# Low parts of weights taken from GpSimd after the first stage, softmax weighting moved to VectorE, three staggered steps in the attentions of a three-layer fp32 block

## The chip, the cores and the metric

One core of a Trainium2 chip runs the whole program in one launch. The metric is the device time in microseconds (us), the median of three runs of the kernel before.

## The reference

256 tokens of width 1024 go through two blocks in fp32. Three attentions and three feed-forward parts are computed, each on a normed residual:

```python
# first block: 16 heads in 8 pairs
y_b = mla_attention(q_nope, q_rope, k_nope, k_rope, v_b)     # 8 heads, 256 keys, causal
y_a = dsa_sparse_attention(...)                              # 8 heads, keys chosen by top-k of an index score, bias by distance
x = x + (gates0 * (y_a @ w_branch_a) + gates1 * (y_b @ w_branch_b)) @ w_out
x = x + square(relu(rmsnorm(x) @ w_ff1)) @ w_ff2             # 4096 wide
# second block, two layers
h = h + swa_sink_mixer(...)     # 16 heads, window of 128, a bias by distance, a sink: P = softmax(S)
h = h + swiglu(...)             # 2816 wide
h = h + nsa_mixer(...)          # 16 heads, three softmaxes each: compressed, selected, window; gated sum
h = h + swiglu(...)
```

## The kernel before

**Weights.** All weights stream through SBUF as 292 slabs of 128 x 1024 fp32, in the order of `_schedule`. Every product of a weight is made of three matmuls of fp32r parts: high part with high part, low with high, high with low. So each slab is split twice before TensorE reads it: its high part (a rounding copy, `hi <- stage`), and its low part (`lo <- stage - hi`, written over the stage). Six double slots of `stage` and eight slots of `hi` turn over. Who splits which slab is set by two sets of slab numbers: `HI_BY_DVE` (VectorE; all others ScalarE) and `LO_BY_POOL` (GpSimd; all others VectorE). Before, VectorE makes the high parts of slabs 20 to 38, 118 to 128, 217, 219, 221 and 223, and GpSimd the low parts of 6 to 38, 112, 114 to 128, the even ones from 194 to 212, and 214 to 225.

**When a split is made.** Each engine's program is an instruction list written out by hand, and runs in order. Class `Splits` keeps its place in it: `slabs.splits(n)` first makes the low parts that are due (`flush`), then up to n high parts of slabs whose slot has been given back; their low parts fall due at the next call. Low parts thus follow one call behind the high ones.

**The three attentions** work on pairs of heads, ten iterations p = 0 to 9 for eight pairs, with the work of neighbouring pairs interleaved. In `pairs` (first and windowed attention) TensorE makes the scores of pair p (`products`), VectorE adds the bias and takes the row maximum (`top`, writes P), ScalarE takes the exponential and its row sum, VectorE inverts the sum, ScalarE multiplies P by it (L1339, the weighting), TensorE transposes the P of pair p - 1 (`turn`), ScalarE copies it to the slot PT (`pt`, L1347), TensorE multiplies the PT of pair p - 2 with the values (`by_values`), and ScalarE and VectorE split the output (`OTH`, `OTL`). Between these stand three calls `fill(p, 0..2)`, which put parts of weight tiles between the steps of the attention: a tile (24 matmuls) has three parts, the first with 6 matmuls, the second with 6, the last with 12; the ScalarE and VectorE programs take the finished tile out of its bank in the third part (`ZR`, `QS` or `AQ <- bank`). Two banks (2 and 3) take turns for these tiles in the first two attentions, one bank (7) in the third; TensorE can't start a tile before VectorE has read the one that last stood in the bank. The fill of the first attention calls `splits(2)` at i = 0 and 2, the fills of the others `splits(1)` at i = 0 and 2.

In the third attention (`nsa_products`, `nsa_turn`, `nsa_values`; scores in `nsa_scores`, weighting on VectorE already in `nsa_weights`, L2249) each pair has six score blocks.

**The bias table of the first attention.** VectorE makes a mask from the top-k at the end of iteration 2 (`MASK`). GpSimd waits for it, then issues eight DMAs that load the bias B1, and then evaluates a flag (`choose`); VectorE's `top` of pair 4 waits for that (`b1`). GpSimd's queue holds the low parts of slabs 24 and on behind it.

Of the kernel before, what the change touches and what calls it, by code (L numbers as in the profile page):

```python
# [318 lines left out]
def _program(nc, io, sched):  # L319
# [70 lines left out]
    PTA = work("PTA", [128, 3, 384], F32, 69632)  # L390
# [30 lines left out]
    PTB = work("PTB", [128, 3, 384], F32, 67008)  # L421
# [11 lines left out]
    PTN = work("PTN", [128, 2, 768], F32, 28672)  # L433
    PCT = work("PCT", [64, 2, 256], F32, 34816)
# [35 lines left out]
    HI_BY_DVE = {*range(20, 39), *range(118, 129), 217, 219, 221, 223}  # L470
    LO_BY_POOL = {*range(6, 39), 112, *range(114, 129), *range(194, 213, 2), *range(214, 226)}
# [25 lines left out]
    def tensor(e):  # L497
# [264 lines left out]
        def pairs(name, P, PT, starts, products, value, fill, also=lambda p: None):  # L762

            def turn(p):
                for h in (2 * p, 2 * p + 1):
                    b = 4 + h % 2
                    clear(b)
                    for part in range(2):
                        q.wait_ge(*at("probabilities", name, h, part))
                    for i, c in enumerate(starts):  # L770
                        x = e.transpose(bank[b][:, 128 * i:128 * i + 128], P[:, h % 4, c:c + 128], idc[:, 0:128])
                    x.then_inc(*up("turned", ("turned", name, h)))
                    free[b] = [("pt", name, h)]

            def by_values(p):
                b, out = 6 + p % 2, bank[6 + p % 2]
                clear(b)
                for o in range(2):
                    q.wait_ge(*at("pt", name, 2 * p + o))
                v = [value(2 * p + o) for o in range(2)]  # L780
                for key in v[0][2]:
                    q.wait_ge(*at(*key))
                for i in range(2):
                    for o, (x, c, _) in enumerate(v):
                        y = e.matmul(out[HALF[o], 128 * i:256], x[:, i, c:c + 64], PT[:, o, 256 * i:256 + 128 * i], start=i == 0, stop=i == 1)
                y.then_inc(*up("values", ("values", name, p)))
                free[b] = [("o high", name, p), ("o low", name, p)]

            for p in range(10):
                if p < 8:  # L790
                    products(p)
                    free[0], free[1] = [("scores read", name, 2 * p)], [("scores read", name, 2 * p + 1)]
                fill(p, 0)
                if p >= 2:
                    by_values(p - 2)
                fill(p, 1)
                if 1 <= p < 9:
                    turn(p - 1)
                fill(p, 2)
                also(p)  # L800
# [211 lines left out]
        def nsa_values(p):  # L1012
            g_, out = p // 4, bank[6]
            clear(6)
            for o in range(2):
                for i in range(2):
                    q.wait_ge(*at("ptn", 2 * p + o, i))
            q.wait_ge(*at("slc values"))
            q.wait_ge(*at("win values"))
            for v, c in ((VS3, 0), (VW3, 384)):  # L1020
                for i in range(2):
                    for o in range(2):
                        x = e.matmul(out[HALF[o], 128 * i:256], v[:, i, 64 * g_:64 * g_ + 64], PTN[:, o, c + 256 * i:c + 256 + 128 * i], start=c + i == 0, stop=False)  # L1023
# [15 lines left out]
        for p in range(10):  # L1039
            if p < 8:  # L1040
                nsa_products(p)
            filler.parts(attention_parts(p, NSA_PARTS)[0])
            if p >= 2:
                nsa_values(p - 2)
            if 1 <= p < 9:
                nsa_turn(2 * p - 2)
            filler.parts(attention_parts(p, NSA_PARTS)[1])
            if 1 <= p < 9:
                nsa_turn(2 * p - 1)
            filler.parts(attention_parts(p, NSA_PARTS)[2])  # L1050
            if p == 0:
                compressed_values()
# [26 lines left out]
    def scalar(e):  # L1079
# [243 lines left out]
        def pairs(name, P, PT, blocks, starts, fill, also=lambda p: None):  # L1323

            for p in range(10):
                if p < 8:
                    for h in (2 * p, 2 * p + 1):
                        for i, (c, w) in enumerate(blocks):
                            exponential(P[:, h % 4, c:c + w], h % 4, i, [("top", name, h, i)], ("exp", name, h, i))
                fill(p, 0)  # L1330
                if p >= 2:
                    q.wait_ge(*at("values", name, p - 2))
                    out_free(name)
                    e.activation(OTH[:, out_tile(name, p - 2), :], bank[6 + p % 2][:, 0:256], ACT.Copy).then_inc(*up("high", ("o high", name, p - 2), ("high", name + " out", out_tile(name, p - 2))))
                if p < 8:
                    for h in (2 * p, 2 * p + 1):
                        q.wait_ge(*at("inverse", name, h))
# [3 lines left out]
                if 1 <= p < 9:  # L1341
                    for o in range(2):
                        h = 2 * p - 2 + o
                        q.wait_ge(*at("turned", name, h))
                        if h >= 2:
                            q.wait_ge(*at("values", name, p - 2))
                        e.activation(PT[:, o, :], bank[4 + o][:, 0:384], ACT.Copy).then_inc(*up("pt", ("pt", name, h)))  # L1347
                fill(p, 2)
                also(p)
# [22 lines left out]

        pairs("first", PA, PTA, ((0, 256), (256, 128)), (256, 0, 128), first_fill, first_also)

# [71 lines left out]
        def attention_fill(p, i, more):  # L1446
            filler.parts(attention_parts(p, more)[i])
            if i != 1:
                slabs.splits(1)
# [6 lines left out]
        pairs("swa", PB, PTB, ((0, 258), (258, 129)), (258, 0, 130), lambda p, i: attention_fill(p, i, SWA_PARTS), swa_also)  # L1456
# [90 lines left out]
        def nsa_turn(h):  # L1547
            q.wait_ge(*at("nsa turned", h, 0))
            if h >= 2:
                q.wait_ge(*at("ptn read", h // 2 - 1))  # L1550
            e.activation(PTN[:, h % 2, 0:512], bank[4][:, :], ACT.Copy).then_inc(*up("pt", ("ptn", h, 0)))
# [5 lines left out]
            e.activation(PTN[:, h % 2, 512:768], bank[5][:, 0:256], ACT.Copy).then_inc(*up("pt", ("ptn", h, 1)))  # L1557

        for p in range(10):
            if p < 8:  # L1560
# [7 lines left out]
            if 1 <= p < 9:  # L1568
                nsa_turn(2 * p - 1)
            attention_fill(p, 2, NSA_PARTS)  # L1570
# [31 lines left out]
    def vector(e):  # L1602
# [367 lines left out]
        def pairs(name, P, blocks, ready, fill, also=lambda p: None):  # L1970
            for p in range(10):
# [9 lines left out]
                if p < 8:  # L1981
                    for h in (2 * p, 2 * p + 1):
                        c = 72 + 6 * (h % 4)
                        q.wait_ge(*at("exp", name, h, 1))
                        e.reciprocal(small[:, c:c + 2], small[:, c:c + 2]).then_inc(*up("step", ("inverse", name, h)))
                if p >= 2:
                    out_low(name, p - 2, 6 + p % 2)
                fill(p, 1)
# [43 lines left out]
        pairs("first", PA, first_blocks, first_ready, first_fill, first_also)  # L2032
# [70 lines left out]
        def attention_fill(p, i, more):  # L2103
# [3 lines left out]
            if i != 1:  # L2107
                slabs.splits(1)
# [5 lines left out]
        pairs("swa", PB, lambda h: ((0, 258, BT[:, h, 0:258]), (258, 129, BT[:, h, 130:259])), swa_ready, lambda p, i: attention_fill(p, i, SWA_PARTS))  # L2114
# [146 lines left out]
        for p in range(10):  # L2261
# [9 lines left out]
            if p < 8:  # L2271
                nsa_weights(2 * p + 1)
            attention_fill(p, 2, NSA_PARTS)
# [20 lines left out]
    def gpsimd(e):  # L2294
# [200 lines left out]
        def attention(more):  # L2495
            for p in range(10):
                for i in range(3):
                    filler.parts(attention_parts(p, more)[i])
                    if i != 1:
                        slabs.splits(1)  # L2500
# [4 lines left out]
        attention(SWA_PARTS)  # L2505
# [44 lines left out]
        attention(NSA_PARTS)  # L2550
# [134 lines left out]
```

## Time and profile before

| | |
|---|---|
| median of 3 runs | 1016.66 us (1015.15 to 1017.91) |
| the profiled execution | 1016.81 us; its span, first to last instruction, 1014.5 us; 2.3 us lie around it |
| TensorE matmul busy | 963.8 us, 95% of the span |
| VectorE / ScalarE / GpSimd busy | 650.6 / 543.5 / 303.6 us |
| mean granted TensorE clock | 0.977 |
| stages, us from the span's start | first projections 0 to 72; first attention 72 to 155; to 400 its output, projection and feed-forward; windowed attention 400 to 462; third-layer projections 662 to 711; third attention 711 to 800 |

Read first where TensorE is not busy, then who released it after each wait, then what that engine did before. Rows of the timeline have start, duration, engine, line and operation, out <- in, the count of instructions merged in a row, and in brackets the idle time ahead with its releaser. L numbers are lines of the kernel.

### The profile page before, as it was taken

What the parts mean: (1) busy time and instruction counts of PE and PEld (TensorE: products, weight loads), DVE (VectorE), ACT (ScalarE), POOL (GpSimd) and SP (SyncE); (2) the same over time, 40 slices, a digit from 0 to 9 for tenths busy, and PEclk for the clock granted to TensorE, in tenths of its full rate; (3) what the DMA queues carried; (4) which work ended last, traced back from release to release, by engine and by line L of the source; (5) the groups of instructions that cost most, each with busy time, mean ns of one, the idle gap of its engine ahead of it and who ended that gap; (6) DMA issues with size and microseconds to landing.
All of it is one profiled execution on the core that took longest, in us unless ns stands there. A gap on an engine that the chain in (4) does not pass through costs nothing.

```text
span 1014.5 us, 19347 instructions
## 1 busy us (share of the span) xinstructions
PE 963.8 (95%) x7816; PEld 929.5 (92%) x7816; DVE 650.6 (64%) x1354; ACT 543.5 (54%) x1136; POOL 303.6 (30%) x202
## 2 busy tenths in 40 slices
PE   7859999999999999899999999998798999999997
PEld 7859899999999999789999999997676999999997
DVE  5897556675555555956865565666997377555552
ACT  6536453565445457676644444456678365444434
POOL 2756674210000015633121111427431022111111
PEclk8979999999999999999999999999799899999999
DMA  8783534495545544216954545455211254554521
GB/s 286 195 184 114 167 126 172 151 271 208 197 169 194 177 167 166 84 45 200 282 189 171 200 170 185 149 208 208 79 47 43 84 202 172 183 192 170 200 88 42
DMA packets 26536, 165.81 MB, mean 163 GB/s; under 512 B 3352, under 2 KB 4248, under 8 KB 8016
## 3 DMA queue, kind: packets, MB, share of 16 engines
q1 hardware_dynamic: 24048, 156.61, 44.1%
q0 software_dynamic: 2400, 7.97, 4.1%
q8 instruction: 62, 1.02, 0.4%
q14 instruction: 26, 0.21, 0.1%
HBM read 161.03 MB, written 3.01 MB: 162 GB/s over the span
## 4 chain that ended last, share of the span: by engine, by line
PE 81%; DVE 9%; ACT 5%; DMA 1%; issue 1%; POOL 1%; SPq 0%; DVEq 0%; POOLq 0%
PE bank L521 12%; PE bank L529 12%; PE bank L525 12%; PE bank L558 9%; PE bank L562 9%; PE bank L560 9%; PE bank L532 4%; PE bank L533 4%; PE bank L538 2%; PE bank L536 2%; DVE DG L1878 1%; ACT PN L1321 1%; DVE PN L2249 1%; DVE hi L1613 1%; PE bank L1023 1%
## 5 line engine op out<-in xcount | busy, mean ns | idle before, releaser
L1089 ACT ACTIVATE hi<-stage 128x1024 fp32r<-128x1024 f32 x257 | 264.6, 1045 | 51.3 <-PE bank L562 47.1
L1620 DVE TENSOR_TENSOR lo<-stage,hi 128x1024 fp32r<-128x1024 f32 x220 | 269.5, 1257 | 12.5 <-ACT hi L1089 12.4
L2302 POOL TENSOR_TENSOR lo<-stage,hi 128x1024 fp32r<-128x1024 f32 (+1 forms) x71 | 177.3, 2516 | 275.3 <-ACT hi L1089 240.7
L558 PE MATMUL bank<-UH,hi 128*128 128x256 f32 x608 | 172.3, 283 | 0.0
L562 PE MATMUL bank<-UL,hi 128*128 128x256 f32 x608 | 172.2, 283 | 0.0
L560 PE MATMUL bank<-UH,lo 128*128 128x256 f32 x608 | 172.1, 283 | 0.0
L521 PE MATMUL bank<-HTH,hi 128*128 128x256 f32 (+1 forms) x1038 | 159.6, 290 | 13.1 <-DVE QS L1709 6.8
L529 PE MATMUL bank<-HTL,hi 128*128 128x256 f32 (+1 forms) x1038 | 157.6, 289 | 0.0
L525 PE MATMUL bank<-HTH,lo 128*128 128x256 f32 (+1 forms) x1038 | 156.5, 287 | 0.2 <-DVE lo L1620 0.2
L521 PEld LDWEIGHTS bank<-HTH,hi 128*128 128x128 f32 (+1 forms) x1038 | 138.8, 193 | 18.3 <-DVE QS L1709 7.6
L2521 POOL TENSOR_TENSOR TH<-TH,RR 128x256 f32<-128x256 f32 x44 | 68.1, 1549 | 279.9 <-DVE TH L2126 279.9
L529 PEld LDWEIGHTS bank<-HTL,hi 128*128 128x128 f32 (+1 forms) x1038 | 139.5, 194 | 2.0 <-issue 1.8
L525 PEld LDWEIGHTS bank<-HTH,lo 128*128 128x128 f32 (+1 forms) x1038 | 138.8, 194 | 1.1 <-issue 0.7
L562 PEld LDWEIGHTS bank<-UL,hi 128*128 128x128 f32 x608 | 116.7, 192 | 0.1
L558 PEld LDWEIGHTS bank<-UH,hi 128*128 128x128 f32 x608 | 116.7, 192 | 0.1
L560 PEld LDWEIGHTS bank<-UH,lo 128*128 128x128 f32 x608 | 116.7, 192 | 0.0
L532 PE MATMUL bank<-HTH,hi 128*128 128x256 f32 (+2 forms) x346 | 98.9, 286 | 0.0
L533 PE MATMUL bank<-HTH,lo 128*128 128x256 f32 (+2 forms) x346 | 98.7, 285 | 0.0
L1397 ACT ACTIVATE UH<-U 128x256 fp32r<-128x256 f32 x76 | 31.7, 417 | 82.8 <-DVE U L2132 81.8
L533 PEld LDWEIGHTS bank<-HTH,lo 128*128 128x128 f32 (+2 forms) x346 | 67.1, 194 | 0.0
L532 PEld LDWEIGHTS bank<-HTH,hi 128*128 128x128 f32 (+2 forms) x346 | 67.1, 194 | 0.0
L2064 DVE TENSOR_TENSOR UL<-U,UH 128x256 fp32r<-128x256 f32 x76 | 32.9, 433 | 51.3 <-ACT UH L1397 51.3
(310 smaller groups left out, 1549.5 us busy)
## 6 DMA issues: line engine op xcount, KB each, us to landing
stage<-in_stream SPq DMA_DIRECT2D x144, 1024.0 KB, 4.8
BT<-scratch POOLq DMA_DIRECT2D x8, 256.0 KB, 15.4
BT<-scratch POOLq DMA_DIRECT2D x4, 512.0 KB, 20.0
stage<-in_stream SPq DMA_DIRECT2D x3, 512.0 KB, 9.6
scratch<-VR POOLq DMA_DIRECT2D x2, 768.0 KB, 21.0
XT<-in_xt SPq DMA_DIRECT2D x4, 256.0 KB, 6.4
B<-scratch POOLq DMA_DIRECT2D x4, 256.0 KB, 5.2
out<-ROWS SPq DMA_DIRECT2D x4, 256.0 KB, 2.4
```

Source lines behind the costliest of these rows:

```text
L521: e.matmul(out, wh[k], rows.high(k0 + k), start=k == 0, stop=False)
L525: e.matmul(out, wl[k], rows.high(k0 + k), start=False, stop=False)
L529: e.matmul(out, wh[k], rows.low(k0 + k), start=False, stop=False)
L532: e.matmul(out, wh[k], rows.high(k0 + k), start=False, stop=False)
L533: e.matmul(out, wl[k], rows.high(k0 + k), start=False, stop=False)
L558: e.matmul(out, hi[:, j % HI_SLOTS, c:c + 128], rows.high(k), start=start and n % 2 == 0, stop=False)
L560: e.matmul(out, lo[:, j // 2 % ST_PAIRS, j % 2, c:c + 128], rows.high(k), start=False, stop=False)
L562: last = e.matmul(out, hi[:, j % HI_SLOTS, c:c + 128], rows.low(k), start=False, stop=stop)
L1089: e.activation(hi[:, j % HI_SLOTS, 0:w], stage[:, j // 2 % ST_PAIRS, j % 2, 0:w], ACT.Copy).then_inc(*up("hi", ("hi", j, 0)))
L1620: e.tensor_tensor(lo[x], stage[x], f32(hi[:, j % HI_SLOTS, 0:sched[j][2]]), ALU.subtract).then_inc(*up("lo", ("lo", j, 0)))
L2302: e.tensor_tensor(lo[x], stage[x], f32(hi[:, j % HI_SLOTS, 0:sched[j][2]]), ALU.subtract).then_inc(*up("lo_pool", ("lo", j, 0)))
L2521: e.tensor_tensor(t, z, ROOT[stage], ALU.mult).then_inc(*up("silu", ("silu scaled", kind, f)))
```

## The change

Slab by slab: `HI_BY_DVE` becomes empty (ScalarE makes all high parts), and GpSimd keeps the low parts of slabs 6 to 19 alone (VectorE makes the rest). In `pairs` the weighting of P moves from ScalarE (two activations for each head) to VectorE (two `tensor_scalar` for each head), right behind the inversion. In all three attentions the order becomes: scores, fill 0, transposes of the pair before, fill 1, values of the pair before that, fill 2; in the third, the first head's transposes stand ahead of the scores. Four PT slots instead of two used ones let the transposed P of a pair stand while the next is written. How many high parts each fill makes is read from a table in the second and third attention.

```diff
-    PTA = work("PTA", [128, 3, 384], F32, 69632)
+    PTA = work("PTA", [128, 4, 384], F32, 66560)
...
-    PTN = work("PTN", [128, 2, 768], F32, 28672)
-    PCT = work("PCT", [64, 2, 256], F32, 34816)
+    PTN = work("PTN", [128, 4, 768], F32, 28672)
+    PCT = work("PCT", [64, 2, 256], F32, 49280)
...
-    HI_BY_DVE = {*range(20, 39), *range(118, 129), 217, 219, 221, 223}
-    LO_BY_POOL = {*range(6, 39), 112, *range(114, 129), *range(194, 213, 2), *range(214, 226)}
+    SWA_SPLITS = ((0, 0, 1),) * 5 + ((0, 1, 1), (0, 1, 1), (1, 1, 1), (1, 1, 1), (1, 1, 1))
+    NSA_SPLITS = ((0, 0, 1),) * 6 + ((0, 1, 1), (0, 1, 1), (1, 1, 1), (1, 1, 1))
+
+    HI_BY_DVE = set()
+    LO_BY_POOL = set(range(6, 20))
# TensorE, pairs
                 fill(p, 0)
+                if 1 <= p < 9:
+                    turn(p - 1)
+                fill(p, 1)
                 if p >= 2:
                     by_values(p - 2)
-                fill(p, 1)
-                if 1 <= p < 9:
-                    turn(p - 1)
                 fill(p, 2)
# TensorE, third attention
         for p in range(10):
+            if 1 <= p < 9:
+                nsa_turn(2 * p - 2)
             if p < 8:
                 nsa_products(p)
             filler.parts(attention_parts(p, NSA_PARTS)[0])
+            if 1 <= p < 9:
+                nsa_turn(2 * p - 1)
+            filler.parts(attention_parts(p, NSA_PARTS)[1])
             if p >= 2:
                 nsa_values(p - 2)
-            if 1 <= p < 9:
-                nsa_turn(2 * p - 2)
-            filler.parts(attention_parts(p, NSA_PARTS)[1])
-            if 1 <= p < 9:
-                nsa_turn(2 * p - 1)
# ScalarE, pairs: the weighting goes
-                        for i, (c, w) in enumerate(((starts[1], starts[2] + 128 - starts[1]), (starts[0], 128))):
-                            e.activation(P[:, h % 4, c:c + w], P[:, h % 4, c:c + w], ACT.Copy, scale=row_stat(h % 4, 1, i)).then_inc(*up("pt", ("probabilities", name, h, i)))
# ScalarE, third attention: the turns stand ahead of each exponential
+            if 1 <= p < 9:
+                nsa_turn(2 * p - 2)
             if p < 8:
                 nsa_exp(2 * p)
-            attention_fill(p, 0, NSA_PARTS)
+            attention_fill(p, 0, NSA_PARTS, NSA_SPLITS)
             if 1 <= p < 9:
-                nsa_turn(2 * p - 2)
-            attention_fill(p, 1, NSA_PARTS)
+                nsa_turn(2 * p - 1)
+            attention_fill(p, 1, NSA_PARTS, NSA_SPLITS)
             if p < 8:
                 nsa_exp(2 * p + 1)
# VectorE, pairs
                         e.reciprocal(small[:, c:c + 2], small[:, c:c + 2]).then_inc(*up("step", ("inverse", name, h)))
+                        q.wait_ge(*at("inverse", name, h))
+                        for i, (c, w) in enumerate(((starts[1], starts[2] + 128 - starts[1]), (starts[0], 128))):
+                            e.tensor_scalar(P[:, h % 4, c:c + w], P[:, h % 4, c:c + w], row_stat(h % 4, 1, i), None, ALU.mult).then_inc(*up("probabilities", ("probabilities", name, h, i)))
+                fill(p, 1)
                 if p >= 2:
                     out_low(name, p - 2, 6 + p % 2)
-                fill(p, 1)
                 fill(p, 2)
# VectorE, third attention
-            attention_fill(p, 0, NSA_PARTS)
+            attention_fill(p, 0, NSA_PARTS, NSA_SPLITS)
+            if p < 8:
+                nsa_weights(2 * p)
+            attention_fill(p, 1, NSA_PARTS, NSA_SPLITS)
             if p >= 2:
                 outs(p - 2)
             if p < 8:
-                nsa_weights(2 * p)
-            attention_fill(p, 1, NSA_PARTS)
-            if p < 8:
                 nsa_weights(2 * p + 1)
```

## Rows read from the trace of the kernel before

**Rows 1.** Windows by stage: length, busy of each engine (instructions), granted clock, DMA, GB/s
```profile
72.00:155.00 83.00, 79.21 (x644) 72.68 (x643) 50.01 (x170) 47.89 (x147) 55.21 (x29) 1.00 0.44 145
...
400.00:462.00 62.00, 55.69 (x448) 49.67 (x447) 44.80 (x117) 44.39 (x136) 32.25 (x14) 0.97 0.26 94
...
662.00:711.00 49.00, 44.28 (x347) 40.81 (x347) 33.78 (x51) 27.88 (x45) 26.34 (x13) 0.97 0.59 214
711.00:800.00 89.00, 77.77 (x606) 65.50 (x605) 67.31 (x352) 59.25 (x241) 25.36 (x11) 0.90 0.14 49
```

**Rows 2.** Waits of TensorE: us in total, times, longest
```profile
PE bank L521 <- DVE QS L1709: 6.8, 4, 4.7
PE bank L785 <- ACT PTB L1347: 5.8, 4, 2.8
...
PE bank L934 <- POOL lo L2302: 2.1, 1, 2.1
...
PE bank L956 <- DVE HE L2200: 1.6, 1, 1.6
```

**Rows 3.** Five lines: ns min/median/max, first and last start
```profile
L1620 DVE TENSOR_TENSOR lo<-stage,hi x220: 710/1218/3405, 14.5 to 987.0; 128x1024 fp32r<-128x1024 f32 x109, 128x544 fp32r<-128x544 f32 x1
...
L1613 DVE CAST hi<-stage x34: 675/684/2867, 83.7 to 751.8; 128x1024 fp32r<-128x1024 f32 x34
...
L2249 DVE TENSOR_SCALAR PN<-PN,small x64: 272/313/2468, 716.9 to 785.5; 128x128 f32<-128x128 f32 x32, 128x256 f32<-128x256 f32 x32
...
L1692 DVE SCALAR_TENSOR_TENSOR XT<-XT,col,RR x8: 459/1718/2358, 410.9 to 427.9; 128x256 f32<-128x256 f32 x8
...
L1089 ACT ACTIVATE hi<-stage x257: 507/1045/1067, 13.4 to 982.8; 128x1024 fp32r<-128x1024 f32 x128, 128x544 fp32r<-128x544 f32 x1
```

**Rows 4.** Timeline of VectorE in the first attention
```profile
80.04 0.21 DVE L1985 RECIPROCAL small<-small 128x2 f32<-128x2 f32 x2
...
82.15 0.42 DVE L1709 TENSOR_TENSOR ZR<-bank,RR 128x256 f32<-128x256 f32 x1 [1.43 <-PE bank L538]
...
83.66 2.05 DVE L1613 CAST hi<-stage 128x1024 fp32r<-128x1024 f32 x2
...
115.32 0.42 DVE L1954 CUSTOM_DVE_ANT_0 PA<-bank,B 128x256 f32<-128x256 f32 x1 [6.53 <-POOL flag L2460]
...
118.29 0.41 DVE L1709 TENSOR_TENSOR ZR<-bank,RR 128x256 f32<-128x256 f32 x1
```

**Rows 5.** Timeline of GpSimd in the first attention
```profile
79.80 4.75 POOL L2302 TENSOR_TENSOR lo<-stage,hi 128x1024 fp32r<-128x1024 f32 x2 [3.47 <-ACT hi L1089]
...
101.46 4.64 POOL L2358 DMA_DIRECT2D B<-scratch  x8 [4.27 <-DVE MASK L2030]
```

**Rows 6.** Timeline of TensorE, windowed attention: scores of pairs 1, 3, 4 and 7
```profile
405.90 0.93 PE L808 MATMUL bank<-KW,QS 64*128 64x258 f32 x8
...
421.02 0.93 PE L808 MATMUL bank<-KW,QS 64*128 64x258 f32 x8
...
426.57 0.93 PE L808 MATMUL bank<-KW,QS 64*128 64x258 f32 x8
...
445.36 0.93 PE L808 MATMUL bank<-KW,QS 64*128 64x258 f32 x8
```

**Rows 7.** Timeline of VectorE in the third attention
```profile
716.85 3.09 DVE L2249 TENSOR_SCALAR PN<-PN,small 128x128 f32<-128x128 f32 x4
...
721.75 0.42 DVE L1709 TENSOR_TENSOR QS<-bank,RR 128x256 f32<-128x256 f32 x1
...
760.45 0.41 DVE L1709 TENSOR_TENSOR QS<-bank,RR 128x256 f32<-128x256 f32 x1
...
769.43 0.42 DVE L1709 TENSOR_TENSOR QS<-bank,RR 128x256 f32<-128x256 f32 x1
...
784.83 1.01 DVE L2249 TENSOR_SCALAR PN<-PN,small 128x128 f32<-128x128 f32 x4
```

**Rows 8.** Windows: one stretch at the lower clock
```profile
704.00:707.40 3.40, 3.40 (x18) 3.40 (x18) 0.56 (x1) 3.40 (x6) 3.07 (x2) 0.50 0.39 166
```

More of the change, by code:

```diff
@@ L420, in _program @@
     PB = work("PB", [128, 4, 388], F32, 59648)
-    PTB = work("PTB", [128, 3, 384], F32, 67008)
+    PTB = work("PTB", [128, 4, 384], F32, 67008)
     TH = work("TH", [128, 2, 2, 256], F32, 40960)
@@ L784, in by_values @@
                     for o, (x, c, _) in enumerate(v):
-                        y = e.matmul(out[HALF[o], 128 * i:256], x[:, i, c:c + 64], PT[:, o, 256 * i:256 + 128 * i], start=i == 0, stop=i == 1)
+                        y = e.matmul(out[HALF[o], 128 * i:256], x[:, i, c:c + 64], PT[:, (2 * p + o) % 4, 256 * i:256 + 128 * i], start=i == 0, stop=i == 1)
                 y.then_inc(*up("values", ("values", name, p)))
@@ L1022, in nsa_values @@
                     for o in range(2):
-                        x = e.matmul(out[HALF[o], 128 * i:256], v[:, i, 64 * g_:64 * g_ + 64], PTN[:, o, c + 256 * i:c + 256 + 128 * i], start=c + i == 0, stop=False)
+                        x = e.matmul(out[HALF[o], 128 * i:256], v[:, i, 64 * g_:64 * g_ + 64], PTN[:, (2 * p + o) % 4, c + 256 * i:c + 256 + 128 * i], start=c + i == 0, stop=False)
             x.then_inc(*up("values", ("ptn read", p)))
@@ L1321, in exponential, with pairs @@
             e.activation(P, P, ACT.Exp, bias=row_stat(slot, 0, i), scale=-1.0, accum_out=row_stat(slot, 1, i)).then_inc(*up("exp", done))
-        def pairs(name, P, PT, blocks, starts, fill, also=lambda p: None):
+        def pairs(name, P, PT, blocks, fill, also=lambda p: None):
             for p in range(10):
@@ L1330, in pairs @@
                 fill(p, 0)
+                if 1 <= p < 9:
+                    for h in (2 * p - 2, 2 * p - 1):
+                        q.wait_ge(*at("turned", name, h))
+                        if h >= 4:
+                            q.wait_ge(*at("values", name, p - 3))
+                        e.activation(PT[:, h % 4, :], bank[4 + h % 2][:, 0:384], ACT.Copy).then_inc(*up("pt", ("pt", name, h)))
+                fill(p, 1)
                 if p >= 2:
@@ L1371, in first_also @@
                 in_halves(("ak",), ZK, 0, AK, ("zk",), 0.125)
-        pairs("first", PA, PTA, ((0, 256), (256, 128)), (256, 0, 128), first_fill, first_also)
+        pairs("first", PA, PTA, ((0, 256), (256, 128)), first_fill, first_also)
         for i in range(8):
@@ L1444, in scalar, with attention_fill @@
                         + [(lambda i: part_of("swa_o", i, early), i) for m in ((4, 6), (0, 2)) for i in range(8 - STAG) for n in m])
-        def attention_fill(p, i, more):
+        def attention_fill(p, i, more, splits):
             filler.parts(attention_parts(p, more)[i])
-            if i != 1:
-                slabs.splits(1)
+            slabs.splits(splits[p][i])
         def swa_also(p):
@@ L1454, in swa_also @@
                 key_head(1)
-        pairs("swa", PB, PTB, ((0, 258), (258, 129)), (258, 0, 130), lambda p, i: attention_fill(p, i, SWA_PARTS), swa_also)
+        pairs("swa", PB, PTB, ((0, 258), (258, 129)), lambda p, i: attention_fill(p, i, SWA_PARTS, SWA_SPLITS), swa_also)
         project("swa_o", early, "mlp2", 4)
@@ L1548, in nsa_turn @@
             q.wait_ge(*at("nsa turned", h, 0))
-            if h >= 2:
-                q.wait_ge(*at("ptn read", h // 2 - 1))
-            e.activation(PTN[:, h % 2, 0:512], bank[4][:, :], ACT.Copy).then_inc(*up("pt", ("ptn", h, 0)))
+            if h >= 4:
+                q.wait_ge(*at("ptn read", h // 2 - 2))
+            e.activation(PTN[:, h % 4, 0:512], bank[4][:, :], ACT.Copy).then_inc(*up("pt", ("ptn", h, 0)))
             q.wait_ge(*at("nsa turned", h, 1))
@@ L1968, in flat_low, with pairs @@
             e.tensor_tensor(FLO[:, kv, :], FL[:, kv, :], f32(FH[:, kv, :]), ALU.subtract).then_inc(*up("low", ("flat low", kv)))
-        def pairs(name, P, blocks, ready, fill, also=lambda p: None):
+        def pairs(name, P, blocks, starts, ready, fill, also=lambda p: None):
             for p in range(10):
@@ L2030, in first_also @@
                 e.scalar_tensor_tensor(MASK[:, :], WKS[:, :], -1e30, causal, ALU.mult, ALU.min).then_inc(*up("step", ("mask",)))
-        pairs("first", PA, first_blocks, first_ready, first_fill, first_also)
+        pairs("first", PA, first_blocks, (256, 0, 128), first_ready, first_fill, first_also)
         assert rounds[0] == 8
@@ L2101, in vector, with attention_fill @@
                         + [(lambda i: part_of("swa_o", i, early), i) for m in ((4, 6), (0, 2)) for i in range(8 - STAG) for n in m])
-        def attention_fill(p, i, more):
+        def attention_fill(p, i, more, splits):
             filler.parts(attention_parts(p, more)[i])
@@ L2106, in attention_fill @@
                 some_later(1)
-            if i != 1:
-                slabs.splits(1)
+            slabs.splits(splits[p][i])
         def swa_ready(p):
@@ L2112, in swa_ready @@
             q.wait_ge(*at("bt"))
-        pairs("swa", PB, lambda h: ((0, 258, BT[:, h, 0:258]), (258, 129, BT[:, h, 130:259])), swa_ready, lambda p, i: attention_fill(p, i, SWA_PARTS))
+        pairs("swa", PB, lambda h: ((0, 258, BT[:, h, 0:258]), (258, 129, BT[:, h, 130:259])), (258, 0, 130), swa_ready, lambda p, i: attention_fill(p, i, SWA_PARTS, SWA_SPLITS))
         some_later(8)
@@ L2268, in vector @@
             if p < 8:
-                nsa_weights(2 * p)
-            attention_fill(p, 1, NSA_PARTS)
-            if p < 8:
                 nsa_weights(2 * p + 1)
-            attention_fill(p, 2, NSA_PARTS)
+            attention_fill(p, 2, NSA_PARTS, NSA_SPLITS)
         project("nsa_o", early, (7, 0, 1, 2), "mlp3", 6)
@@ L2493, in gpsimd, with attention @@
             slabs.splits(1)
-        def attention(more):
+        def attention(more, splits):
             for p in range(10):
@@ L2498, in attention @@
                     filler.parts(attention_parts(p, more)[i])
-                    if i != 1:
-                        slabs.splits(1)
+                    slabs.splits(splits[p][i])
         early = {}
@@ L2504, in gpsimd @@
                         + [(lambda i: part_of("swa_o", i, early), i) for m in ((4, 6), (0, 2)) for i in range(8 - STAG) for n in m])
-        attention(SWA_PARTS)
+        attention(SWA_PARTS, SWA_SPLITS)
         project("swa_o", early, "mlp2")
@@ L2549, in gpsimd @@
                         + [(lambda i: part_of("nsa_o", i, early), i) for n in (0, 2, 4) for i in range(8 - STAG)])
-        attention(NSA_PARTS)
+        attention(NSA_PARTS, NSA_SPLITS)
         project("nsa_o", early, "mlp3")
```

18 lines of the change are left out of this document (4 added, 14 removed).

## The prediction, made before the changed kernel ran

> **What bounds the kernel now.** First the windows by stage [rows 1]: TensorE is full but for 3.8 us in the first attention, 6.3 in the windowed one, 4.7 in the projections of the third layer and 11.2 in the third attention. Everywhere between 155 and 662 us but for the windowed attention it is full, so what a stage loses or wins there goes into the total whole. The clock column gives a second loss in the last three stages (0.97, 0.97, 0.90): one stretch of 3.4 us at the lower of the two levels, 1.2 GHz, stands by itself [rows 8], with 18 matmuls where a full stretch has twice as many; it follows two waits of 2.1 and 1.6 us. So an avoided wait can give back 1.7 us more than its length.
>
> Then the waits of TensorE [rows 2]. In the windowed attention it waits 5.8 us for ScalarE's PT copies; those stand in ScalarE's queue behind the weighting, and that behind VectorE. In the third layer it waits for one low part by GpSimd (2.1), for a tiny VectorE operation `HE` (1.6), and 6.8 us for VectorE's `QS` (4.7 of it once).
>
> Then why VectorE is late [rows 3]. Three of its operations have two durations: the cast of a slab 684 ns or up to 2867, the `tensor_scalar` of P 313 or up to 2468, the XT scaling 459 or a median of 1718. The long ones all overlap a low part by GpSimd (2.4 us each, [rows 5]): VectorE stands until GpSimd's operation is done. VectorE's sources in PSUM (`top`, `ZR`) don't show it.
>
> **What the change does, first attention.** It takes GpSimd out of the later stages, but here slabs 18 and 19 are still its own, at 79.80 to 84.55 [rows 5], and VectorE's new weighting of pair 0 would start right behind the inversion at 80.04 [rows 4]. So I expect the first `tensor_scalar` to stand until 82.2 and the second until 84.6; with the other two it is done at 85.5 (four take 1.01, [rows 7]), 5.2 later. The wait of 1.43 and the two casts of 2.05 that followed [rows 4] are no longer there: +1.8 for `top` of pair 1. In iteration 1 VectorE makes two low parts (1.22 each, [rows 3]) where it made two casts (0.68 each), and 1.0 of weighting: +2.1. The same in iteration 2, of which about 0.9 fills a wait for the exponential (an estimate): +1.2. Nothing of this was done by VectorE before, and all of it is ahead of the mask: GpSimd waits for the mask with nothing else to do (4.27 idle, [rows 5]), so mask, bias DMAs, flag and `top` of pair 4 are 5.1 us later. VectorE already stood 6.53 us for the flag [rows 4]; the whole chain shifts. Behind `top` of pair 4 stand two low parts and the weighting, 2.4 + 1.0, of which 1.5 replace waits and the OTL step that moves behind: the tile read `ZR` (118.29) comes another 1.9 later. TensorE's next tile needs that bank. It is full from there on, so it gets nothing back: **+7.0**. Bounds: 3, if pair 0's weighting doesn't meet GpSimd and the waits absorb more; 10, if ScalarE's 19 more high parts (1.05 each, [rows 3]) hold up the exponentials as well. With waits over 2 us in it, a stretch at the lower clock is likely: **+1** (0 to 3.4, two stretches as in [rows 8]).
>
> The Trainium skill has a rule that speaks against this move. By the Trainium skill, "SBUF — State Buffer", "SBUF: two separate sides", VectorE and GpSimd share a port pair that is an exclusive lock, and a VectorE operation in a two-port mode also keeps GpSimd from writing the descriptors of its own DMAs. The trace agrees on the lock (684 against 2867 ns); by the second half the eight bias DMAs could stretch under pair 3's weighting. No row here shows that, and the sum leaves it out.
>
> **Windowed attention.** GpSimd's 14 low parts go to VectorE (16 us by [rows 3]), the weighting too (8 pairs at 1.0). In return the 11 casts go (0.68 alone, up to 2.87), and the eight XT steps fall from 1.72 to 0.46, 10 us. VectorE, busy 44.8 of 62 [rows 1], stays about there. Before, pairs took 5.55 us where nothing was late (421.02 to 426.57, [rows 6]); the six from pair 1 to pair 7 took 39.5 (405.90 to 445.36). The PT copy of a pair now has a whole iteration, and P is needed one fill earlier, which VectorE alone can meet (weighting done some 4 us behind the scores). Six pairs at 5.55 are 33.3: **-6.2**. Bounds: -2, if low parts ahead of the weighting hold up the transposes; -8, with the lighter last pairs.
>
> **Ahead of the third attention.** The low part of a `cw1` slab comes 1.2 us after its high part instead of 2.4: -1.2 of the 2.1. `HE` no longer stands behind GpSimd: -1.6. The slow stretch goes: -1.7. **-4.5**; bounds -1 and -5.
>
> **Third attention.** Start: pair 0's weighting falls from 3.09 to 1.01 [rows 7], its gelu steps by about 1.1 (as `HE` in [rows 2], an estimate), and one low part, 1.2, comes in ahead: -2.0 for the first `QS`. Five iterations take 47.7 us (721.75 to 769.43, [rows 7]); the last of them, without a collision, takes 8.98. That is not VectorE's work but a loop: exponential of the first head, turn copies, exponential of the second head on ScalarE, then weighting and `QS`. The new order keeps this loop, now with a low part (1.2) in VectorE's gap, so I take 9.0 for each: 45.0, -2.7. In iterations 6 and 7 the table asks for two splits each: a high part (1.05) stands on ScalarE ahead of the second exponential, and a second low part (1.2) on VectorE. 9.0 - 0.4 (no `QS`) + 1.05 + 1.2 = 10.8, and 9.6 up to the last weighting: 20.4 against 16.4 (769.43 to 785.84): +4.0. TensorE waits for that weighting either way. **-0.7**; bounds -6 (table harmless) and +5 (the loop gets longer by the low part).
>
> **Sum.** 7.0 + 1 - 6.2 - 4.5 - 0.7 = -3.4. The span of 1014.5 becomes 1011.1, the execution 1013.4 with the 2.3 around it; the profiled execution, 1016.81, stood 0.15 above the median: 1013.3.
>
> **The rivals.**
> - *The first attention doesn't pay.* If the collision with slabs 18 and 19 is short or the mask's lateness is covered, it costs 2 instead of 8, and the rest stands: 1007.3. For it: VectorE has 33 us idle of 83 there [rows 1]. Against: none of it lies ahead of the mask.
> - *The bias chain decides, and the time is above before.* One place: the mask of iteration 2. It costs 10 and the lower clock twice, 13; the stages behind give back 7 instead of 11.4, as the third attention's end takes its part: +6, 1022. From a loss of 11.4 in the first attention on, this is the outcome. Against: it needs ScalarE late too, which is idle for half of that stage.
> - *VectorE becomes the bound in the attentions.* It gets 57 low parts (70 us by [rows 3]) and the weighting. In the third attention it is busy 67.3 of 89 [rows 1], of which some 8 were collisions (four, 2.1 each). If each low part adds its 1.2 to the nine-us loop, five iterations give back nothing, the windowed one 4: +2, 1018.
> - *Nothing to measure.* The moved work costs as much as the collisions did: 1016.
>
> **How the numbers follow.** Forecast's case 0.50 (1010 to 1017), first rival 0.17, second 0.10, third 0.13, fourth 0.10. A measurement of this kernel tells 0.3%, 3 us, from no change. The forecast lies just beyond that, so its half gives 0.29 faster, 0.20 same, 0.01 slower; the first rival is faster, the second slower, the third 0.08 slower and 0.05 same, the fourth 0.08 same, 0.02 slower. Faster 0.46, same 0.33, slower 0.21. The range takes in the first rival and the third, 1007 to 1020.
>
> **What would show it.** In the profile after: weighting of pair 0 beside GpSimd's last two low parts with a duration over 2 us; mask at 106 us instead of 101, flag at 120; a TensorE wait for `ZR` behind it; no wait for PTB in the windowed attention and pairs at 5.55 us; no cast or `tensor_scalar` over 0.4 us behind 85 us; `cw1` without its wait and no slow stretch near 700 us; third attention's iterations at 9.0, the last two near 10. The forecast is wrong if the mask isn't later, or if those iterations come out at 10 or at 8.5.

## The result, and the profile after

The changed kernel takes 1009.38 us (median of 6 runs, 1008.40 to 1010.87), the kernel before 1015.12 (6 runs, 1013.54 to 1017.91): ratio 0.9942, 95% interval 0.9925 to 0.9959, 5.7 us faster. The profiled span falls from 1014.5 to 1007.0 us. The forecast was 1013.3 with a range of 1007 to 1020: the sign and the range hold, but the time lies just below the forecast's own case (1010 to 1017) and nearer to its first rival's 1007.3, -3.4 became -7.5 in the span, and the terms behind it are further off than their sum.

Windows of the kernel after, same stages and columns as [rows 1]:

```profile
72.00:155.00 83.00, 75.30 (x578) 69.35 (x577) 59.05 (x194) 49.80 (x125) 11.85 (x12) 0.94 0.41 133
...
400.00:462.00 62.00, 59.54 (x473) 52.32 (x474) 46.05 (x155) 45.42 (x122) 0.00 (x0) 0.97 0.28 96
662.00:711.00 49.00, 48.46 (x408) 46.41 (x407) 35.86 (x67) 30.80 (x53) 4.18 (x7) 1.00 0.62 218
711.00:800.00 89.00, 79.36 (x652) 67.24 (x652) 72.10 (x362) 67.52 (x251) 0.00 (x0) 0.96 0.17 62
```

The first attention has become worse (TensorE busy 75.3 instead of 79.2, clock 0.94 instead of 1.00), the three later stages better. TensorE's longest waits, the counterpart of [rows 2]:

```profile
PE bank L734 <- DVE DG L1874: 11.8, 1, 11.8
PE bank L1002 <- DVE PN L2247: 5.9, 3, 2.6
PE bank L524 <- DVE ZR L1705: 4.1, 3, 2.5
...
PE bank L1002 <- ACT PTN L1547: 2.9, 2, 2.7
```

The waits for PTB, for GpSimd's `lo`, for `HE` and nearly all of the one for `QS` are gone. New or longer are those for `ZR` (2.5 of it in the first attention) and for `PN` and PTN: `PN` 2.6 once at the start of the third attention, 2.5 and PTN 2.7 at its end, where before had one of 2.6 for PTN. The first row, `DG`, was there before with 11.9 us. VectorE and GpSimd in the first attention, against [rows 4, 5]:

```profile
79.19 4.41 DVE L1984 TENSOR_SCALAR PA<-PA,small 128x256 f32<-128x256 f32 x2
...
83.71 0.55 DVE L1984 TENSOR_SCALAR PA<-PA,small 128x256 f32<-128x256 f32 x2
...
118.56 0.42 DVE L1950 CUSTOM_DVE_ANT_0 PA<-bank,B 128x256 f32<-128x256 f32 x1 [7.97 <-POOL flag L2458]
...
119.68 2.35 DVE L1616 TENSOR_TENSOR lo<-stage,hi 128x1024 fp32r<-128x1024 f32 x2
...
122.14 0.55 DVE L1984 TENSOR_SCALAR PA<-PA,small 128x256 f32<-128x256 f32 x2
...
123.27 0.42 DVE L1705 TENSOR_TENSOR ZR<-bank,RR 128x256 f32<-128x256 f32 x1
```
```profile
78.76 4.76 POOL L2300 TENSOR_TENSOR lo<-stage,hi 128x1024 fp32r<-128x1024 f32 x2 [3.46 <-ACT hi L1092]
105.14 4.63 POOL L2356 DMA_DIRECT2D B<-scratch  x8 [21.62 <-DVE MASK L2029]
```

Pair 0's weighting stands beside GpSimd's two low parts until 83.6, as forecast. Behind `top` of pair 4 come the two low parts and the weighting, and `ZR` is read 4.7 us later than `top`, where it was 3.0. TensorE waits 2.49 us for it, and has the second window below at the lower level (1.2 GHz); the first is the stretch near 700 us that was slow in [rows 8], now at full clock, with 30 matmuls where before had 18:

```profile
703.99:707.39 3.40, 3.40 (x30) 3.40 (x30) 1.75 (x3) 2.15 (x4) 0.00 (x0) 1.00 0.88 337
...
122.20:129.00 6.80, 5.26 (x24) 5.26 (x25) 5.88 (x20) 5.17 (x14) 0.00 (x0) 0.50 0.12 49
```

VectorE's `QS` in the third attention, the counterpart of [rows 7]: five iterations take 41.36 us instead of 47.68, from here on the last weighting 19.1 instead of 16.4.

```profile
718.89 0.41 DVE L1705 TENSOR_TENSOR QS<-bank,RR 128x256 f32<-128x256 f32 x1
...
760.25 0.42 DVE L1705 TENSOR_TENSOR QS<-bank,RR 128x256 f32<-128x256 f32 x1
...
778.36 1.01 DVE L2247 TENSOR_SCALAR PN<-PN,small 128x128 f32<-128x128 f32 x4
```

**The span cut at marks.** For all kernels the trace was cut at TensorE's first matmul of the first attention's scores (A), of the first merged accumulation behind it (B), of the windowed scores (C), of the last windowed values (D), of `cw1` (E), of the third attention's scores (F) and of the last pair's values there (G). D is the start of the last pair's values too. Lengths in us, each from one profiled execution, so a span with the 2 us around it can lie up to 2.7 us from the median:

| kernel | to A | A-B | B-C | C-D | D-E | E-F | F-G | G-end | span | median us |
|---|---|---|---|---|---|---|---|---|---|---|
| before | 72.4 | 105.9 | 223.5 | 55.5 | 228.5 | 25.0 | 86.0 | 217.8 | 1014.5 | 1015.1 |
| after | 71.3 | 115.7 | 225.5 | 51.6 | 226.8 | 18.2 | 80.8 | 217.0 | 1007.0 | 1009.4 |
| e1 sets alone | 71.4 | 107.3 | 224.4 | 54.7 | 228.2 | 18.3 | 86.2 | 217.7 | 1008.1 | 1010.0 |
| e9 order alone* | 71.2 | 107.1 | 223.5 | 59.0 | 227.1 | 25.0 | 90.4 | 217.0 | 1020.3 | 1021.6 |
| e2 both* | 71.1 | 107.9 | 224.4 | 51.6 | 227.7 | 18.3 | 81.8 | 217.0 | 999.7 | 999.3 |
| e12 e2, windowed order, weighting old | 70.9 | 106.0 | 225.4 | 57.2 | 228.2 | 18.3 | 80.6 | 217.0 | 1003.6 | 1005.7 |
| e5 old order, sets of after | 72.7 | 108.4 | 224.4 | 51.6 | 226.7 | 18.3 | 80.4 | 217.0 | 999.5 | 1001.5 |
| e10 e5, VectorE weights | 72.4 | 114.7 | 224.4 | 51.7 | 226.7 | 18.3 | 80.5 | 217.0 | 1005.6 | 1006.3 |
| e6 new order, sets of before | 70.1 | 125.2 | 224.4 | 51.6 | 227.3 | 18.2 | 81.8 | 217.0 | 1015.8 | 1016.8 |
| e3 GpSimd 6 to 17 | 70.1 | 116.2 | 224.4 | 51.6 | 226.7 | 18.3 | 80.8 | 217.0 | 1005.1 | 1009.5 |
| e4 even table | 71.2 | 115.7 | 225.6 | 51.6 | 226.7 | 18.3 | 80.7 | 217.0 | 1006.7 | 1008.6 |
| e7 e2, slabs 9 to 15 to VectorE | 69.1 | 106.6 | 225.5 | 51.6 | 226.7 | 18.3 | 80.8 | 217.0 | 995.6 | 998.9 |
| e8 e2, later table | 69.8 | 107.1 | 224.4 | 51.6 | 226.7 | 18.3 | 77.1 | 217.0 | 992.0 | 996.5 |
| e11 e7 and e8 | 69.8 | 106.6 | 225.4 | 51.7 | 226.7 | 18.3 | 75.6 | 217.0 | 991.1 | 993.9 |

\* with the first attention as before; e5, e10 and e6 vary the first attention of after and nothing else. A stage that two kernels share has the same length within some 2 us (2.9 in "to A", which runs from 69.8 to 72.7 in kernels that are the same there), most within 0.2: the stages pass their times on, and can be added. The kernel before was timed beside each group of runs, at 1014.6 to 1015.5; ratios are to that.

### The profile page after: what moved, and what is told of

It is laid out like the page before. It is cut to its first block, busy times and chain, and to the rows that moved or that the text cites. A ratio compares the mean times of both kernels' runs of the same rounds, so it can differ in the third digit from the quotient of the medians.

```text
span 1007.0 us, 19387 instructions
## 1 busy us (share of the span) xinstructions
PE 961.3 (95%) x7816; PEld 926.9 (92%) x7816; DVE 666.0 (66%) x1441; ACT 552.3 (55%) x1106; POOL 160.1 (16%) x145
## 4 chain that ended last, share of the span: by engine, by line
PE 79%; DVE 11%; ACT 6%; issue 1%; DMA 1%; POOL 0%; SPq 0%; DVEq 0%; POOLq 0%; ACTq 0%
PE bank L524 12%; PE bank L528 12%; PE bank L532 11%; PE bank L561 9%; PE bank L565 9%; PE bank L563 9%; PE bank L536 3%; PE bank L535 3%; DVE lo L1616 2%; ACT PN L1324 2%; PE bank L541 2%; PE bank L539 2%; DVE DG L1874 1%; ACT hi L1092 1%; DVE PN L1950 1%
## 5 line engine op out<-in xcount | busy, mean ns | idle before, releaser
L1616 DVE TENSOR_TENSOR lo<-stage,hi 128x1024 fp32r<-128x1024 f32 x277 | 330.3, 1223 | 11.9 <-ACT hi L1092 11.8
L1092 ACT ACTIVATE hi<-stage 128x1024 fp32r<-128x1024 f32 x291 | 299.3, 1045 | 59.9 <-PE bank L565 52.3
L2312 POOL TENSOR_TENSOR SQ<-SQ 128x256 f32<-128x256 f32 x40 | 34.2, 863 | 424.2 <-ACT SQ L1108 423.1
L1394 ACT ACTIVATE UH<-U 128x256 fp32r<-128x256 f32 x76 | 31.7, 418 | 82.2 <-DVE U L2130 81.2
L2063 DVE TENSOR_TENSOR UL<-U,UH 128x256 fp32r<-128x256 f32 x76 | 32.3, 425 | 52.7 <-ACT UH L1394 52.7
L535 PEld LDWEIGHTS bank<-HTH,hi 128*128 128x128 f32 (+2 forms) x346 | 66.4, 192 | 0.0
```

The source lines that it names most:

```text
L535: e.matmul(out, wh[k], rows.high(k0 + k), start=False, stop=False)
L1092: e.activation(hi[:, j % HI_SLOTS, 0:w], stage[:, j // 2 % ST_PAIRS, j % 2, 0:w], ACT.Copy).then_inc(*up("hi", ("hi", j, 0)))
L1616: e.tensor_tensor(lo[x], stage[x], f32(hi[:, j % HI_SLOTS, 0:sched[j][2]]), ALU.subtract).then_inc(*up("lo", ("lo", j, 0)))
L2312: e.tensor_tensor(sq[:, 0, :], sq[:, 0, :], sq[:, k, :], ALU.add).then_inc(*up("sums", ("squares so far", stage, c, k), *[("squares", stag ...
```

## The experiments

**e1, the sets alone.** The kernel before, with

```
HI_BY_DVE = set(range(20, 39)); LO_BY_POOL = set(range(6, 39))
```

> The kernel before, with its own order, its weighting on ScalarE and its even splits; only the sets change, and only behind the first attention: GpSimd makes no low part and VectorE no high part from slab 111 on. Theory (the collisions are what cost before, outside the first attention): cw1 and HE lose their waits and the slow stretch near 704 us (-4.5 to -6.7), pair 0 of the third attention starts 2 us earlier, its last two iterations don't get longer; together -8 to -11, 1004 to 1007 us. On the third attention's period the theories part: by the loop of the prediction it is 9.0 us per pair also without collisions, since the order is the old one; by the rival (TensorE itself is the bound once nothing collides) it is 8.4. In the windowed attention the order theory expects waits for PTB to stay and six pairs near 37 us; the rival, 33.4. If collisions were harmless, 1015.

Measured 1009.95 us, ratio 0.9952 (0.9939 to 0.9966): less gain than the expected 1004 to 1007. E-F gets all that it gets in after, 6.7 us. F-G gets nothing, C-D 0.9: TensorE's waits for PTB stay (5.4 us), and `QS` comes every 10.03 us three times, then 9.20 and 8.98. The loop theory is right that the old order doesn't reach TensorE's 8.4, and too short by 1.0 for most periods. The rows of e1 also tell which half of a split costs: the periods of 10.03 hold two low and two high parts, that of 9.20 two low parts and one high part, that of 8.98 one of each. So ScalarE's high part is worth 0.8 there, VectorE's low part 0.2.

**e9, the order alone.** First attention as before, then order, slots, weighting and table of the change, with the two sets of before unchanged.

> The kernel with the first attention as before, and in the two later attentions the order, slots, weighting and table of the change, but GpSimd and VectorE making the same low and high parts as before (the four sets of before unchanged): the order alone, where e1 was the sets alone (1010) and both together gave 999.3. Theory (the two halves add: the sets are worth 6.7 in the projections ahead of the third attention, the order 4 to 5 in each attention): 1005 to 1007. Rival (they need each other: weighting on VectorE behind GpSimd's low parts stands up to 2.4 us per operation, so the new order alone loses what it gains): 1011 to 1016, pairs of the third attention at 9.5 or more, those of the windowed one at 6 or more.

Measured 1021.64 us, ratio 1.0060 (1.0045 to 1.0076): slower than before, and slower than the rival's 1016. C-D takes 59.0, F-G 90.4. In the windowed attention the six pairs take 33.5, not 6 us each: the loss stands at its end, where TensorE waits 5.7 us once for a weighting that meets a low part (2.46 us long) and runs at the lower level from 449.7 to 456.5. VectorE's rows in the third attention:

```profile
751.90 0.42 DVE L1724 TENSOR_TENSOR QS<-bank,RR 128x256 f32<-128x256 f32 x1
...
759.54 3.10 DVE L2270 TENSOR_SCALAR PN<-PN,small 128x128 f32<-128x128 f32 x4
...
762.83 0.41 DVE L1724 TENSOR_TENSOR QS<-bank,RR 128x256 f32<-128x256 f32 x1
```

A period with a collision takes 10.93 us (3.10 for four operations that take 1.01 alone), one without 8.21. The two halves of the change don't add, they need each other (e2 has both).

**e2, both, with the first attention as before.** Weighting on ScalarE, old order, GpSimd low parts 6 to 38, VectorE high parts 20 to 38, all inside `if name == "first"`.

> The kernel after, with the first attention as it was: weighting on ScalarE, old order, GpSimd making low parts 6 to 38 and VectorE the high parts 20 to 38. Theory (the change costs 9 to 10 us there and everything behind passes it on, since TensorE is full): 999 to 1001 us, mask near 100.6, first merged accumulation 178 us instead of 187. Rival (the lateness would be taken up behind anyway, or the first attention doesn't pay): 1006 to 1009.

Measured 999.31 us, ratio 0.9848 (0.9833 to 0.9863). Theory holds: of the 10 us between the medians of after and this kernel, 8.0 are there at B (179.0 instead of 187.0).

**e5, e10, e6: what costs in the first attention.** All three are the kernel after with a part of the change undone there.

```
e5   order old, weighting on ScalarE, sets of after
e10  order old, weighting on VectorE, sets of after
e6   order new, weighting on VectorE, LO_BY_POOL 6 to 38, HI_BY_DVE 20 to 38
```

> The kernel after, with the first attention's order and its weighting on ScalarE as before, but the sets of after (GpSimd 6 to 19, VectorE all other low parts, ScalarE all high parts). The change there costs some 9.5 us in the first attention. Theory of the prediction (cost of the weighting on VectorE ahead of the mask, 1.0 to 1.8 per iteration, and of low parts for casts, 1.1 per iteration, add up): this kernel gets back about half, 1004 to 1006, mask 2 to 3 us earlier than in after. Rival (the table read behind the top of pair 4 is all of it, due to two low parts in VectorE's queue): 1008 to 1010, no gain. Second rival (the weighting is all of it): 1000.

> The kernel after, with the first attention's old order of fills, transposes, copies and values, but the weighting on VectorE and the sets of after: it differs from e5 (1001.5) in the weighting's engine alone, and from after (1009.4) in the order alone. Theory of the prediction (the weighting's 1.0 to 1.2 per iteration in VectorE's queue ahead of mask and ahead of the read behind the top of pair 4 is what costs): 1005 to 1009. Rival (the order costs: transposes and values one fill later or earlier on banks that TensorE needs): 1000 to 1003.

> The complement: the kernel after with its own order and weighting on VectorE in the first attention, but the sets of before there (GpSimd makes low parts 6 to 38, VectorE the high parts 20 to 38). Theory (sum of parts): 1004 to 1006 with mask 1 to 2 us earlier. Rival (each tensor_scalar of the weighting now stands behind a low part of GpSimd, up to 2.4 us each): 1009 to 1014, weighting of a pair 3 to 5 us instead of 1.0, transposes late.

Measured 1001.48, 1006.33 and 1016.83 us. The traces, from the scores of pair 1 to B, give 96.4 us in before, 96.9 in e2, 98.9 in e5, 105.2 in e10 and 104.7 in after. So low parts for casts cost 2.0 us there, and the weighting on VectorE 6.3 (4.9 between the medians). The order costs nothing there: B stands at 187.1 in e10 and at 187.0 in after. The medians of e10 and after do differ, by 3.1 us (ratios 0.9906 and 0.9942, whose intervals all but touch); of that the two profiled spans show 1.4, 1.1 of it in B-C, where after has a stretch at the lower level (402.1 to 405.5) and e10 none. The medians of e2 and e5 differ by 2.2, their ratios (0.9848, 0.9853) by 0.5, so the 2.0 rest on the traces alone. e5 came out better than its forecast, between theory and second rival.

Mask behind the scores of pair 1: 18.7 in before, 17.5 in e5, 22.5 in e10, 22.0 in after. So the low parts, which the forecast charged with 1.1 per iteration, don't make the mask late; the weighting does. In e6 the mechanism of its rival is seen, though the time is above it: the two weightings of one iteration take 3.03 and this, TensorE waits 7.3 and 6.0 us, and runs at the lower level from 121.1 to 138.2.

```profile
128.20 4.53 DVE L1984 TENSOR_SCALAR PA<-PA,small 128x256 f32<-128x256 f32 x2
```

**e3, slabs 18 and 19 to VectorE** (`LO_BY_POOL = set(range(6, 18))`).

> The kernel after, with slabs 18 and 19 given to VectorE: nothing of GpSimd's lies beside the weighting of pair 0. Theory (the collision of 4.4 us is worth +1.8 in the first attention, as predicted, less the two low parts of 1.2 each that VectorE gets): mask and flag 1 to 2 us earlier, time -0.5 to -2: 1007.5 to 1009. Rival (the collision sets the whole chain): -4, 1005. Second rival (the two low parts cost as much as the collision): no change, and the top of pair 1 comes at the same time.

Measured 1009.49 us (ratio 0.9960, 0.9944 to 0.9976), the same as after; mask 22.05 behind the scores of pair 1 instead of 21.98, `top` of pair 1 5.2 instead of 5.1. The second rival: two low parts of 1.2 cost VectorE what the collision did.

**e4, even table in the third attention** (`NSA_SPLITS = ((1, 0, 1),) * 10`).

> The kernel after, with one split ahead of the first and one ahead of the last fill in each iteration of the third attention instead of its table (one split at the end of each of six iterations, then two, two, three, three). Theory of the prediction (the table's second split in iterations 6 and 7 costs 4 us at the end, and the low part isn't on the loop): the end gets 2 to 4 us shorter, the period stays 8.4, 1006 to 1007.5 us. Rival (VectorE's low part ahead of the weighting is on the loop): periods of 9.2 or more instead of 8.4, +4 to +6, 1014.

Measured 1008.56 us (ratio to before 0.9938, 0.9919 to 0.9957, after's 0.9942). As a time neither holds, but both were right, each for its half: from the second `QS` three periods are 9.2 us instead of 8.2, and from the last `QS` to the last weighting it is 16.0 instead of 19.1. ScalarE shows why, with a high part between the exponentials of the two heads:

```profile
732.22 1.04 ACT L1092 ACTIVATE hi<-stage 128x1024 fp32r<-128x1024 f32 x1
733.17 0.57 ACT L1547 ACTIVATE PTN<-bank 128x512 f32<-128x512 f32 x1
...
734.17 0.50 ACT L1324 ACTIVATE PN<-PN,small 128x256 f32<-128x256 f32 x1
```

**e12, the windowed attention in its old order**, with its weighting on ScalarE, everything else as e2.

> The kernel with the first attention as before (e2, 999.3), and the windowed attention too with its old order and its weighting on ScalarE; its table (one split in each of five iterations, then two and three), the sets and the third attention stay as changed. Six pairs took 33.4 us in after and e2, 39.5 in before, 38.0 in e1, where the sets alone were changed. Theory (the weighting on ScalarE ahead of the PT copies is what makes TensorE wait): six pairs at 37 to 38 again, the wait for PTB back with 3 us or more, 1002.5 to 1004. Rival (one high part less on ScalarE per iteration, by the table, is enough): 33.4 to 34.5, no wait for PTB, 999 to 1000.5.

Measured 1005.7 us, ratio 0.9913 (0.9893 to 0.9932). The six pairs take 34.1, as the rival had it, but the waits are back, 4.7 of them behind the six pairs, a stretch at the lower level begins in the last (449.7 to 456.6), and C-D takes 57.2 instead of 51.6:

```profile
PE bank L788 <- ACT PTB L1343: 7.1, 4, 3.2
```

So the windowed gain is the order and the weighting together (this run doesn't part them), given that nothing collides.

**e7, e8, e11: towards a version that beats both.** All start from e2.

```
e7   LO_BY_POOL = {6, 7, 8} and 16 to 38
e8   NSA_SPLITS = ((0, 0, 1),) * 8 + ((1, 1, 1), (1, 1, 1))
e11  both
```

> The kernel with the first attention as before (999.3 us), and in it slabs 9 to 15 given from GpSimd to VectorE. In every kernel so far VectorE's DG (128x512) takes 13.9 us while GpSimd makes seven low parts back to back (43 to 59 us), TensorE waits 11.8 us for it and then runs 13.7 us at the lower level. Theory (VectorE stands until the whole train of GpSimd's operations has passed): DG takes 0.6 us, TensorE's wait falls to between 0 and 4 us (VectorE has seven low parts of 1.2 itself), with the slow stretch gone or shorter: 986 to 992 us. Rival (the high parts or the slabs' DMAs set the time there, and the wait only changes its name): 997 to 1000.

> The kernel with the first attention as before (999.3 us), and in it the table of the third attention later: one split in iterations 0 to 7 and three each in 8 and 9. Theory (the second split in iterations 6 and 7 stands ahead of the last weightings, as the even table's end was 3 us shorter): the two waits of 2.5 and 2.7 us at the end shrink by 2 to 4 together, 996 to 998 us. Rival (slabs are then missing behind, in the projection of the third attention: waits for hi or lo of 2 us or more): 999 to 1002.

> First attention as before, without GpSimd's low parts of slabs 9 to 15, with the later table: e7 (-0.4 against 999.3) and e8 (-2.8) add to 995 to 997; if the wait for the DMA of the rotated keys gives back less beside them, 992.

Measured 998.89, 996.54 and 993.91 us. e8's theory holds: `QS` to last weighting 16.2 instead of 19.2, F-G 77.1. In e7 VectorE's row and TensorE's wait are:

```profile
45.20 0.69 DVE L1893 TENSOR_TENSOR DG<-idc,small 128x512 f32<-128x512 f32 x1
```
```profile
PE bank L825 <- DMA K<-KR: 6.8, 1, 6.8
PE bank L524 <- ACT CTH L1297: 3.4, 1, 3.4
```

The 11.8 us wait is gone, and the rival is right all the same: TensorE now waits for `CTH` and for the transfer of the rotated keys, 10.3 together. A comes at 69.1, 2 us earlier than in e2, but e8 reaches it at 69.8 with the long wait. Nor is the lower level gone: in e2 it lasts from 50.2 to 63.9, 9.4 us of it inside the wait, in e7 from 52.7 to 59.6 and from 66.4 to 73.2. e11 came out faster than the 995 to 997 expected. It has the lowest median of this study, ratio 0.9798 (0.9780 to 0.9816), 21 us under before, but isn't told apart from e8 (0.9804, 0.9785 to 0.9822).

## Why the prediction held, and where its steps failed

- **First attention, +7.0 and +1.** Measured: A to B 9.8 longer; from the scores of pair 1, 8.4. The size is right by bounds, the working only in part. Mask 104.3, flag 118.4 instead of 106 and 120. Against before the tops of pairs 1 and 2 and the mask come 0.6, 2.7 and 3.7 us later; the forecast had 1.8, 3.9 and 5.1, so its first step was too large and the other two held. The collision was there (4.41 us) but cost no more than two low parts (e3). The `ZR` read behind `top` of pair 4 comes 5.0 later, not 7.0. The rest came behind it, where the forecast put nothing but the clock: up to B TensorE is idle 7.0 us from the scores of pair 1 on instead of 1.7 (1.4 of it a wait for `OTH` at 164.3) and works 3.1 longer. The term for the clock was too small: the window at 122.2 has 5.26 us of work at half speed, some 2.6 lost.
- **Windowed attention, -6.2.** The six pairs fell from 39.46 to 33.37 us, 5.56 each: the mechanism and its size hold. Of the gain, C-D shows 3.9 and D-E 1.8, and B-C takes back 2.0. Of that, 1.1 is a stretch at the lower level from 402.1 to 405.5: kernels with such a stretch near the end of B-C take 225.4 to 225.6 there, those with the changed sets and no stretch 224.4. The other 0.9 comes with the sets (e1 224.4, e9 223.5). Net -3.7.
- **Ahead of the third attention, -4.5.** Measured -6.7, all from the sets (e1: 18.3 as in after). From E to F TensorE has no gap left in after; in before it was idle for 4.0 us there (the windows' lengths less its busy time) and lost 1.7 in the slow stretch. So the wait for the low part went whole, 2.1, where the forecast took off 1.2 of it, and some 0.3 of small ones with it; 1.0 of the 6.7 stays unaccounted.
- **Third attention, -0.7.** Measured -5.2 from F to G. This step failed: "The new order keeps this loop ... so I take 9.0 for each". The iterations take 8.2 to 8.4 us, so five give 6.3 and not 2.7; the forecast had itself named 8.5 as a sign of being wrong. Its start gave 1.2 instead of 2.0. The table had been costed only where it adds splits (iterations 6 and 7), not where it takes one away: with two splits per period VectorE's `QS` comes every 10.0 us in the old order (e1) and 9.2 in the new (e4), with one every 9.0 and 8.2. So a split is worth 1.0 and the order 0.8 per period. The row of 8.98 in [rows 7], on which the forecast built, was measured where few splits were left. TensorE's scores come every 8.4 us, with no gap: here it is the bound itself. The term for the end, +4.0, measured +2.7 (19.1 against 16.4), and e8 shows that it was avoidable.
- **The sum.** It held its range in part by luck: the first attention cost 1.8 us more than forecast and the windowed one gave 2.5 less, the two later stages 6.7 more; 1.8 more lie ahead of A and behind G, where the forecast had no term and "to A" varies by more than that.
- **The rivals.** "Nothing to measure" is excluded by the interval. "VectorE becomes the bound" doesn't hold: 72 busy of 89, and one low part per iteration fits. "The bias chain decides" was near in place, not in size: behind that stage the kernel was 8.8 us late, and all that follows gave back 16.3. "The first attention doesn't pay" gave 1007.3, near the time, for the wrong reason.
- **The skill's rule** on the shared port pair (the Trainium skill, "SBUF — State Buffer", "SBUF: two separate sides"): the lock is seen where a cast, a `tensor_scalar` or a `tensor_tensor` on SBUF meets a low part, but not on every VectorE operation there: a `MATCH_REPLACE8` of 128x256 in SBUF takes 0.41 us at 83.08 in before, beside GpSimd's two low parts, as it does without one. Its second half, that VectorE's operations keep GpSimd from writing DMA descriptors, shows nothing here: the eight bias DMAs take 4.63 us to issue with two low parts and pair 3's weighting on VectorE beside them, and 4.64 before without [rows 5]; from mask to flag it is 14.2 and 14.6.

Open is where the other 1.7 us between the medians of e10 and after lie, and so whether the order costs anything in the first attention: the traces up to B show nothing. Only argued is the account of the 6.7 us by single operations; that the sets cause them is shown.

## What to carry to other kernels

Two engines that lock each other out turn work that is moved between engines into an interaction: here, with the first attention left as before, the new order without the new sets cost 6.4 us (e9), the sets without the order gave 4.7 (e1), both together 15.3 (e2). Cost an edit per stage, and undo it in the stage where it doesn't pay. When a table moves work, price the places that it leaves as well as those that it fills.

## What the runs showed of the hardware

- VectorE doesn't wait for one GpSimd operation but can stand through a whole train of them: `DG`, 0.69 us alone, takes 13.88 in after while GpSimd makes seven low parts back to back (16.2 us); with those seven on VectorE it takes 0.69 (e7).
- The same wait of TensorE for `Q`, 2.11 us long, was followed by a stretch at the lower level in after (it ended at 76.3; 77.8 to 81.2 was at 1.2 GHz) and by none in that window in e5 and e10 (it ended at 77.7 and 77.4; e10 has one later, 86.3 to 89.7). All three reach the scores of pair 1 near 82 us, so a start 1 us earlier was worth nothing.
